# Post-norm sums of squares: the eighth square is summed by TensorE on top of the accumulator of seven

## What is computed

```python
x = x + rms_norm(mixer(rms_norm(x, norm_mix_pre)) @ w_out, norm_mix_post)
x = x + rms_norm(memory_attention(rms_norm(x, norm_mem_pre), mem) @ w_mo, norm_mem_post)
x = x + rms_norm(conv_mlp(rms_norm(x, norm_ffn_pre)) @ w_down, norm_ffn_post)
```

```python
x = x + g1 * rms_norm(mixer(modulate(rms_norm(x, g0), sh1, sc1)) @ w_out, norm_g[1])
x = x + g2 * rms_norm(squared_relu_mlp(modulate(rms_norm(x, g2n), sh2, sc2)), norm_g[3])
```

## Time and profile before

| what | value |
|---|---|
| median of 3 runs | 3715.53 us (3714.56 to 3715.6) |
| the profiled execution's own time | 3715.64 us |
| its span, first to last instruction | 3713.4 us |
| PE busy | 3564.8 us (96% of the span) |
| DVE busy, ACT busy | 2028.9 us (55%), 1417.1 us (38%) |
| the chain that ended last | PE 84%, DVE 7%, ACT 5%, issue 2%, DVE's queue 1% |
| mean granted TensorE clock | 0.992 |

### The profile page before, as it was taken

One profiled execution on the slowest core, in us unless ns is written; L12 is line 12 of the kernel. 1 busy time (PEld: TensorE's weight loads), 2 busy tenths in 40 slices (PEclk: granted clock), 3 DMA queues, 4 the chain that ended last, 5 costly groups with the idle time before them and its releaser, 6 DMA issues.

```text
span 3713.4 us, 51728 instructions
## 1 busy us (share of the span) xinstructions
PE 3564.8 (96%) x19164; PEld 2928.4 (79%) x19164; DVE 2028.9 (55%) x3322; ACT 1417.1 (38%) x2192; POOL 241.6 (7%) x384
## 2 busy tenths in 40 slices
PE   8999999999999999999999888999999998899998
PEld 6788877878787888788778776788888887678886
DVE  5634457787764355587784465443233444644445
ACT  3344354232324534522233366432122334743222
POOL 0000000001000000000000052000000002610000
PEclk9999999999999999999999999999999999999999
DMA  3222223446322233244541102111111121112222
GB/s 140 90 74 94 94 91 109 146 141 200 117 96 76 74 107 108 74 142 146 193 156 57 46 2 43 46 57 62 63 62 63 56 74 51 31 52 80 96 96 85
DMA packets 113072, 333.15 MB, mean 90 GB/s; under 512 B 32792, under 2 KB 33688, under 8 KB 112408
## 3 DMA queue, kind: packets, MB, share of 16 engines
q1 hardware_dynamic: 74112, 265.23, 21.3%
q0 software_dynamic: 14400, 52.44, 4.3%
q10 hardware_dynamic: 24408, 13.46, 1.6%
HBM read 328.99 MB, written 6.00 MB: 90 GB/s over the span
## 4 chain that ended last, share of the span: by engine, by line
PE 84%; DVE 7%; ACT 5%; issue 2%; DVEq 1%; POOL 0%; POOLq 0%; ACTq 0%; DMA 0%; SPq 0%
PE PS L632 14%; PE PS L633 13%; PE PS L634 13%; PE PS L1134 11%; PE PS L1135 10%; PE PS L1137 10%; PE PS L1275 1%; PE PS L751 1%; PE PS L816 1%; DVE WL L2165 1%; ACT PB L1899 1%; ACT FULL_P L1899 1%; PE PS L828 1%; DVE MX L2688 1%; PE PS L845 1%
## 5 line engine op out<-in xcount | busy, mean ns | idle before, releaser
L2165 DVE TENSOR_TENSOR WL<-RAW,WH 128x1024 fp32r<-128x1024 f32 x486 | 594.4, 1224 | 558.7 <-ACT WH L1503 555.2
L1503 ACT ACTIVATE WH<-RAW 128x1024 fp32r<-128x1024 f32 x486 | 512.9, 1056 | 786.5 <-PE PS L634 420.7
L632 PE MATMUL PS<-HHI,WH 128*128 128x512 f32 x1584 | 635.8, 401 | 10.2 <-DVE WL L2165 4.4
L633 PE MATMUL PS<-HLO,WH 128*128 128x512 f32 x1584 | 622.1, 393 | 0.0
L634 PE MATMUL PS<-HHI,WL 128*128 128x512 f32 x1584 | 618.4, 390 | 0.0
L1134 PE MATMUL PS<-H2HI,WH 128*128 128x512 f32 (+1 forms) x1288 | 453.1, 352 | 2.2 <-DVE TMP L2885 2.2
L1135 PE MATMUL PS<-H2LO,WH 128*128 128x512 f32 (+1 forms) x1288 | 430.4, 350 | 0.0
L1137 PE MATMUL PS<-H2HI,WL 128*128 128x512 f32 (+1 forms) x1288 | 372.9, 350 | 0.0
L632 PEld LDWEIGHTS PS<-HHI,WH 128*128 128x128 f32 x1584 | 297.5, 188 | 94.8 <-issue 15.8
L634 PEld LDWEIGHTS PS<-HHI,WL 128*128 128x128 f32 x1584 | 297.4, 188 | 65.8
L633 PEld LDWEIGHTS PS<-HLO,WH 128*128 128x128 f32 x1584 | 297.8, 188 | 63.2 <-issue 4.3
(11 more groups left out here) (402 smaller groups left out, 5768.4 us busy)
## 6 DMA issues: line engine op xcount, KB each, us to landing
RAW<-in_stream SPq DMA_DIRECT2D x494, 512.0 KB, 3.2
MODW<-in_modw POOLq DMA_DIRECT2D x96, 512.0 KB, 3.6
bias_rows<-in_rpb ACTq DMA_DIRECT2D x8, 476.2 KB, 6.1
X<-in_x SPq DMA_DIRECT2D x4, 512.0 KB, 5.5
MEM<-in_mem ACTq DMA_DIRECT2D x2, 1024.0 KB, 4.8
CROW<-in_crow POOLq DMA_DIRECT2D x4, 512.0 KB, 4.8
BIAS<-bias_rows ACTq DMA_DIRECT2D x8, 224.0 KB, 4.9
GRID<-bias_rows ACTq DMA_DIRECT2D x8, 224.0 KB, 5.1
```

Source lines behind the costliest of these rows:

```text
L632: nc.tensor.matmul(out, WH[:, slot, b * P:(b + 1) * P], hi, start=start, stop=False)
L633: nc.tensor.matmul(out, WH[:, slot, b * P:(b + 1) * P], lo, start=False, stop=False)
L1503: A(WH[:, d, :] if home is None else home[0][:], RAW[:, s, :], ACT.Copy).then_inc(high_split, 1)
L2165: TT(low_at, RAW[:, s, :], high_at.bitcast(F32), ALU.subtract).then_inc(split_ready, 1)
```

## The change

1. `statistics` no longer runs the eight filler products. It waits for one addition fewer (six, which cover seven squares), multiplies ACC by ones without closing the sum, then waits for a new semaphore, `last_squared`, and multiplies the eighth square by ones on top of it.
2. DVE no longer adds the eighth square at any of the twelve places. After w_down the addition of the seventh square is moved from the end of the seventh block's round to the end of the eighth's.
3. ACT squares each output block before it copies it, and the bank is handed back by the copy instead of the square. Only the eighth square counts up `last_squared`.
4. The two table loads (L1707, L1828) are issued ahead of the eight squares instead of behind them.

```diff
             def statistics(n):
-                keep_clock(8)
-                m.add("sqt", KB - 1)
+                cuts = [(c0, min(c0 + T, n)) for c0 in range(0, n, T)]
+                m.add("sqt", KB - 2)
                 pe.wait_ge(sq_taken, m.at("sqt"))
-                for c0 in range(0, n, T):
-                    c1 = min(c0 + T, n)
-                    nc.tensor.matmul(FLAT[:, 6 * T + c0:6 * T + c1], ONES[:], ACC[:, c0:c1], start=True, stop=True).then_inc(stat_done, 1)
+                for c0, c1 in cuts:
+                    nc.tensor.matmul(FLAT[:, 6 * T + c0:6 * T + c1], ONES[:], ACC[:, c0:c1], start=True, stop=False, skip_group_check=True)
+                m.add("last")
+                pe.wait_ge(last_squared, m.at("last"))
+                for c0, c1 in cuts:
+                    nc.tensor.matmul(FLAT[:, 6 * T + c0:6 * T + c1], ONES[:], SQ[:, (KB - 1) % 2, c0:c1], start=False, stop=True,
+                                     skip_group_check=True).then_inc(stat_done, 1)
...
             def of_y(k, dst, n):
                 p = unit_wait()
                 m.add(f"use{p}")
-                A(Y[:, k, :], bank(3 * p), ACT.Copy)
-                A(dst[:, 0:n], bank(3 * p), ACT.Square, scale=D ** -0.5).then_inc(taken[p], 1)
+                square = A(dst[:, 0:n], bank(3 * p), ACT.Square, scale=D ** -0.5)
+                if k == KB - 1:
+                    square.then_inc(last_squared, 1)
+                A(Y[:, k, :], bank(3 * p), ACT.Copy).then_inc(taken[p], 1)
                 split_high()
...
+                act.preload_act_table_set("natural_log_exp_and_others")
                 squares(of_y, T)
-                act.preload_act_table_set("natural_log_exp_and_others")
                 root(T)
...
             def add_squares(k, n, arrived):
                 if k == 0:
+                    return
+                if k == KB - 1:
                     return
...
                 if add:
-                    for b in (KB - 2, KB - 1):
-                        add_squares(b, T, sq_arrived)
+                    add_squares(KB - 2, T, sq_arrived)
...
                             u += 1
-                    add_squares(k, T, y_arrived)
+                    if k != KB - 2:
+                        add_squares(min(k, KB - 2), T, y_arrived)
...
                     if k:
                         add_squares(k - 1, n2, y_square_arrived)
-                add_squares(KB - 1, n2, y_square_arrived)
                 split_low()
```

More of the change, by code:

```diff
@@ L485, in build @@
         RAW_LAPS = tuple(f"lap{s}" for s in range(RAW_SLOTS))
-        MARKS = ("sum", "of", "qkh", "qks", "vh", "vs", "r", "sc", "comb", "ptl", "modw0", "modw1", "crow", "modu", "relu", "y", "hsq", "bias", "in2", "units", "use0", "use1", "consts", "mem", "pool", "x", "sq", "sqt", "stat", "root", "val", "hi", "lo", "pooled", "mixed",
+        MARKS = ("sum", "last", "of", "qkh", "qks", "vh", "vs", "r", "sc", "comb", "ptl", "modw0", "modw1", "crow", "modu", "relu", "y", "hsq", "bias", "in2", "units", "use0", "use1", "consts", "mem", "pool", "x", "sq", "sqt", "stat", "root", "val", "hi", "lo", "pooled", "mixed",
                  "vt", "vtr", "roped", "s", "max", "exp", "pt", "pts", "merge", "gate", "ab", "conv", "silu", "otd", "inverse", "sums", "w") + RAW_LAPS
@@ L1553, in of_y, with of_x @@
                 m.add(f"use{p}")
-                A(Y[:, k, :], bank(3 * p), ACT.Copy)
-                A(dst[:, 0:n], bank(3 * p), ACT.Square, scale=D ** -0.5).then_inc(taken[p], 1)
+                square = A(dst[:, 0:n], bank(3 * p), ACT.Square, scale=D ** -0.5)
+                if k == KB - 1:
+                    square.then_inc(last_squared, 1)
+                A(Y[:, k, :], bank(3 * p), ACT.Copy).then_inc(taken[p], 1)
                 split_high()
-            def of_x(k, dst, n):
+            def of_x(k, dst, n, last=True):
                 m.add("x")
                 act.wait_ge(x_ready, m.at("x"))
-                A(dst[:, 0:n], X[:, k, :], ACT.Square, scale=D ** -0.5).then_inc(sq_ready, 1)
+                square = A(dst[:, 0:n], X[:, k, :], ACT.Square, scale=D ** -0.5)
+                square.then_inc(last_squared if last and k == KB - 1 else sq_ready, 1)
             def high(dst, src, sem_=None):
@@ L1760, in of_mo @@
                     p = (m.n["units"] - 1) % SLOTS
-                    A(Y[:, k, :], bank(3 * p + k % 2), ACT.Copy)
-                    sq = A(dst[:, 0:n], bank(3 * p + k % 2), ACT.Square, scale=D ** -0.5)
-                    sq.then_inc(taken[p] if k % 2 else sq_ready, 1)
+                    square = A(dst[:, 0:n], bank(3 * p + k % 2), ACT.Square, scale=D ** -0.5)
+                    if k == KB - 1:
+                        square.then_inc(last_squared, 1)
+                    A(Y[:, k, :], bank(3 * p + k % 2), ACT.Copy).then_inc(taken[p] if k % 2 else sq_ready, 1)
                     if k % 2:
@@ L1818, in of_down @@
                     m.add(f"use{k % 2}")
-                    A(Y[:, k, :], bank(3 * (k % 2)), ACT.Copy)
-                    A(dst[:, 0:n], bank(3 * (k % 2)), ACT.Square, scale=D ** -0.5).then_inc(taken[k % 2], 1)
+                    square = A(dst[:, 0:n], bank(3 * (k % 2)), ACT.Square, scale=D ** -0.5)
+                    if k == KB - 1:
+                        square.then_inc(last_squared, 1)
+                    A(Y[:, k, :], bank(3 * (k % 2)), ACT.Copy).then_inc(taken[k % 2], 1)
                     if k == KB - 1:
@@ L2081, in of_y2 @@
                     m.add(f"use{p}")
-                    A(Y2[:, k, 0:n], FLAT[:, 3 * p * T:3 * p * T + n], ACT.Copy)
-                    A(dst[:, 0:n], FLAT[:, 3 * p * T:3 * p * T + n], ACT.Square, scale=D ** -0.5).then_inc(taken[p], 1)
+                    square = A(dst[:, 0:n], FLAT[:, 3 * p * T:3 * p * T + n], ACT.Square, scale=D ** -0.5)
+                    if k == KB - 1:
+                        square.then_inc(last_squared, 1)
+                    A(Y2[:, k, 0:n], FLAT[:, 3 * p * T:3 * p * T + n], ACT.Copy).then_inc(taken[p], 1)
                     split_high()
@@ L2143, in _ @@
                     act.wait_ge(taken[p], m.at(f"use{p}", 1))
-                    A(dst[:, 0:n2], Y2[:, k, 0:n2], ACT.Square, scale=D ** -0.5).then_inc(y_squared, 1)
-                m.add("sqt", KB - 1)
+                    A(dst[:, 0:n2], Y2[:, k, 0:n2], ACT.Square, scale=D ** -0.5).then_inc(last_squared if k == KB - 1 else y_squared, 1)
+                m.add("sqt", KB - 2)
                 roots_y()
@@ L2464, in _ @@
                     split_low()
+                m.add("use1")
                 root_inverse(T)
```

15 lines of the change are left out of this document (9 added, 6 removed).

## The result

The changed kernel takes 3720.74 us (median of 20 runs, 3717.18 to 3724.39), the kernel before 3713.46 (median of 20 on the same chip, 3709.7 to 3717.69). The ratio is 1.0018, with an interval of 1.0011 to 1.0025. The forecast was 3716.5, in a range of 3711.5 to 3721.0: the time lies inside, 0.3 us from its upper end. The difference of about 7 us is small, but its interval, 4 to 9 us, does not reach zero. The profiled execution took 3720.85 with a span of 3719.0, against 3715.64 and 3713.4. So the two traces show +5.6 us of span, and the medians +7.3.

A forecast was written before the change was run, and what follows sets the result against it. PE was taken as the bound, busy 96% of the span, so only seams between stages could move. Seams -2.9 us and clock +1.7 and +2.3 gave +1.1 on 3715.64: 3716.5 us, range 3711.5 to 3721.

The forecast's parts named there:

- w_out of the first block, -1.26 each: After w_out, block one, both layers: no table load before the logarithm, next unit 1.26 us earlier, -2.5 in all.
- The stage that follows is tied to both.: After w_out, block one: the next stage follows both ACT's weight split and PE's next unit, taken as 1.26 us earlier.
- Keys and values +0.07, w_mo -0.12, at full clock: Additions come last there: one addition goes, one product comes, +0.07 us and -0.12 us at each of two places.
- w_out of the second block -1.24 and -0.98, MLP +0.24 and 0: Second block: logarithm after w_out 1.2 and 1.0 us earlier; after the MLP +0.2 us, last place zero.
- w_down +0.86 each: After w_down, two places: the moved seventh addition ends as late as before, the second product adds 0.86 us, +1.7 in all.
- the clock, +4.0: Without fillers PE idles and its clock falls: +1.7 us at keys and values of layer one, +2.3 at five other places.
- one and a half falls at five places: w_mo twice, w_down twice, one MLP: one and a half clock falls at 1.5 us each, +2.3 us.
- Sum at unchanged clock -2.9: All twelve places together, without any change of PE's clock: 2.9 us faster.
- The clock holding (3712.6): Rival: idle times at the seams bring no new clock falls, -2.9 us, 3712.6; chance 0.25.
- The clock falling everywhere (3726.8): Rival: PE's clock falls at keys and values, w_mo, w_down and the MLP, +11.2 us, 3726.8; chance 0.05.
- The saving at all twelve places: Rival: an addition of 0.79 and a copy's lead of 0.50 us saved at each place, 3697.5; chance 0.03.
- PE waiting for the eighth square: Rival: the eighth square is late and PE waits; at four places the gain shrinks by 1 us, inside the forecast's range.

The follow-up runs named there:

- a_tables_back: The changed kernel with the two table loads behind the squares again: 3726.15 us, ratio 1.0027 to the kernel before.
- a_fill_all: The changed kernel with the eight fillers back at all twelve places: 3717.17 us, ratio 1.0013 to the kernel before.
- a_fill_late: The changed kernel with eight fillers back at keys and values, w_mo, w_down and MLP, none at w_out: 3712.62 us, ratio 0.9997 to the kernel before.
- b_acts: The kernel before with only squares ahead of copies and table loads ahead of the squares: 3715.55 us, ratio 1.0002.
- b_nofill: The kernel before without its eight filler products ahead of each of the twelve sums, nothing else changed: 3721.12 us against 3713.93, ratio 1.0019.
- a_add7: The changed kernel with the seventh addition after w_down back in its own round, the sum in another bank: 3711.58 us, ratio 0.9997 to the kernel before.
- best: a_add7 plus eight fillers at the keys and values, w_mo and the MLP: 3708.82 us, ratio 0.9984 to the kernel before.
- best_held: The kernel best with 14 fillers instead of 8 after keys and values and 12 more ahead of w_down: 3702.18 us, ratio 0.9968 to the kernel before.
- best_held_2: The same kernel as best_held, run again beside b_held: 3703.07 us, ratio 0.9970 to the kernel before.
- b_held: The kernel before with only more fillers, 14 instead of 8 after keys and values and 12 ahead of w_down: 3708.77 us, ratio 0.9983.

## Why the prediction was right in its range, and off in one term

That the time fell inside the range is in part luck. The forecast was counted from a profiled execution of 3715.64, near the median of three runs, 3715.53; the median of twenty is 3713.46. Counted as a difference, the forecast was +1.1 with a range from -4.0 to +5.5, and the measured +7.3 lies outside. The starting point, 2 us too high, made up for it.

One view was misread, without entering a sum: the 26.7 us of the earlier trace rows are not how much PE waits for ACC in all. They add PE's 12.2 us and 14.5 us of PEld, which is why they count 24 waits at twelve places.

- **w_out of the first block, -1.26 each.** Right: the seams are 1.42 shorter. ACT's split is last, the table load is gone from there, and no cost of the load ahead of the first output block shows. a_tables_back gives the 1.42 back.
- **"The stage that follows is tied to both."** Counted from PE's last unit, the root came 1.42 earlier and the stage ended 1.20 earlier in both layers. The forecast was 1.26, PE's early start. That the numbers agree does not make it the cause: in a_tables_back PE starts as early, and most of the gain is gone.
- **Keys and values +0.07, w_mo -0.12, at full clock.** Right to a hundredth or two: +0.07 or +0.08 and -0.12 or -0.13 in every profile in which the clock held, except in layer two of the keys and values. There the fall of the kernel before had 0.6 in its seam, which is gone where the clock holds.
- **w_out of the second block -1.24 and -0.98, MLP +0.24 and 0.** Right at the seams: -1.38 and -1.11 or -1.12, +0.24 and -0.05. The fall 50 us behind the first, some 1.5 us, was not foreseen.
- **w_down +0.86 each.** Right for the product, short for the seam. In layer two of a_fill_all the seam is 0.85 longer. But a_fill_late, whose pair has fillers ahead of it, still shows +1.99 and +1.94. The other 1.1 is DVE's wait for the last modulation weights, 0.93 and 1.00 in that profile. The same wait stands in b_acts, which changes nothing there:

```profile
961.44 1.23 DVE L2153 CUSTOM_DVE_ANT_0 PS<-MODW,CROW 128x1024 f32<-128x1024 f32 x1 [0.84 <-DMA MODW<-in_modw]
...
1919.45 1.23 DVE L2153 CUSTOM_DVE_ANT_0 PS<-MODW,CROW 128x1024 f32<-128x1024 f32 x1 [0.91 <-DMA MODW<-in_modw]
```

  So the wait does not need the move of the addition. Nine of the twelve profiles have the wait in at least one layer (0.15 to 1.12 us), and the profile of before, from which I read, is one of the three without. It explains about 1 us in each of these seams of the traces. Kernels with and without the change show it; whether it is more frequent in one of them is not shown.
- **The step that failed: the clock, +4.0.** Sum at unchanged clock -2.9, clock +4.0, together +1.1; measured +7.3. The first number holds roughly: the full-clock seams give -3.5 without the transfer's wait (four w_out places -5.3, keys and values +0.14, w_mo -0.24, w_down +1.7, MLP +0.2), about -1.6 with the fall behind w_out and the 0.2 that each keys-and-values stage does not pass on; a_fill_late as a whole came out at -1.3 in medians. The second is too small by about half: 8.6 us by a_fill_late against the changed kernel, 7.2 by b_nofill. Two of its parts were mis-sized.

  First, the number of falls. The prediction called an idle time of 2.1 to 2.6 us "as open as after 2.46, once in two", and then counted one and a half falls at five places, since the shorter three "are less likely". In the three profiles that have such places unfilled (after, a_tables_back, a_add7) 7 of 13 fell: three of six after the shortest wait, 1.96, two of four after w_down, where the two longest waits (3.82 and 3.63) fell and 2.86 and 2.99 held, and two of three after the MLP. Once in two was a fair reading, and the discount was without ground.

  Second, the keys and values. All six such pairs without fillers fell, as forecast. But the earlier trace rows does not show a loss of 1.7 us in layer two of the kernel before: its seam is 0.65 longer than that of layer one, and the stage behind it is no longer than in kernels without the fall. With two products in the pair a fall costs 1.6 to 1.7, so layer one lost 1.6, and layer two, put at nothing, 1.05.

  As an estimate from these counts and seams, 2.7 falls at 1.5 and 2.6 for the keys and values make 6.6 us in place of the 4.0.
- **The rivals.** The clock holding (3712.6) was tried by a_fill_late. Its 3712.62 agrees by the luck of the starting point; as a difference it is -1.3, against -2.9. The clock falling everywhere (3726.8) was put at 7.4 us and more if four of the five places fell besides both of the keys and values. Just that happened in the profile after, and the kernel measured +7.3: counted as a difference, the rival with a chance of 0.05 (+11.2) came nearer than the forecast (+1.1). The saving at all twelve places did not happen; w_down is the one place where a different edit brings it. PE waiting for the eighth square: the view of the second product's line has 2.1 us of such idle time in three places,

```profile
  ACT SQ L1558: 1.4, 2
  ACT SQ L2092: 0.7, 1
```

  but all of it is idle time of the weight loads (PEld) while PE is still at the first product. PE's own rows have none, and at these three places, all w_out, ACT's split comes last in any case.
- **What is still open.** What decides in an execution whether the clock falls after a given wait, or whether the last modulation weights come late, was not found, nor was the share of each single place in the 8.6 us measured: every number for one place comes from one execution.

## What to carry to other kernels

Dummy products that are "off the path" can be part of the path wherever the engine would idle for some 2 us in their place. Before taking them away, ask place by place whether they hold back work (here w_out, where it paid 1.4 us each) or fill a wait that stays (here keys and values, w_mo, w_down, MLP, where it cost some 8.6 us in all). And where a sum waits for an addition that stands behind unrelated work on its engine, move the addition forward and let the reader of the sum take the wait, by giving the sum a bank of its own: that was worth 4.1 us where the clock was held elsewhere (best against a_fill_late) and 9.6 where it was not (a_add7 against the changed kernel), more than the addition that was saved. Last, count a forecast as a difference from a well measured start: here three runs put the start 2 us too high.

## What the runs showed of the hardware that I had not expected

TensorE's clock went to its lower level after only 1.96 us of idle time (w_mo, both layers of the changed kernel, 0.51 and 0.50), and stayed at 1.00 through another idle time of 2.86 (w_down, layer one). In a_add7 the same 1.96 us at w_mo were followed by 1.00 in both layers. Eight dummy products of 128 columns (recorded as sixteen, 1.95 us) ahead of the wait went with a clock of 1.00 in every w_mo pair of the fillers' kernels, where 1.16 or less was left idle; at the keys and values of a_fill_late they left 1.68 idle and the clock held, where in the kernel before 2.46 were left and it fell in one layer of two. The Trainium skill, "TensorE: Matmul & The Clock Gate", "HAM oscillation", tells of a kernel in which every group of products starts at half rate because of the wait ahead of it. The falls at six seams of the changed kernel agree with that, and the pairs that held after 2.86 and, in a_add7, after 1.96 show that it is not so every time.

A change in one place seems to move falls at another. The wait of 2.15 us in the MLP of the second block's first layer is the same in all twelve profiles; the clock falls behind it in all seven with a short w_out seam ahead and in none of the five with the long one. Why is not shown.

The runs of best_held and best_held_2 scatter less than the others: 3.1 us in six runs and 4.3 in nine, against 6.8 to 13.1 in the eight to twenty runs of each other kernel that was compared with the kernel before. Holding the clock alone doesn't explain it, since b_held, with the highest mean clock of all (0.995), has 8.1 in eleven.

The last transfer of modulation weights ahead of w_down's end took 3.4 to 3.6 us from issue to landing in the profile of before and up to 4.7 in others, for the same 512 KB. The page's medians over all 96 such transfers are 3.6 before and, after the change,

```profile
MODW<-in_modw POOLq DMA_DIRECT2D x96, 512.0 KB, 4.6
```

The longer median, 4.5 or 4.6, appears with four kernels: the changed one, b_nofill, a_tables_back and a_add7. The other eight have 3.6 or 3.7. No edit touches the transfer itself, but these four are the ones that have no fillers ahead of the sums, and all the others have some. How the two are connected is not shown. It is not the main part of what the missing fillers cost: DVE's waits for these weights add up to 4.4 us in the profile of the changed kernel, and to 4.5 in that of best_held_2, one of the two fastest.
